# Routing, ranking and gathering tile by tile, and releasing the first expert weight slots in quarters

## The chip, the cores and the metric

The kernel runs on one core of one Trainium2 chip. The metric is the time of one execution on the device in microseconds (us); lower is better. The core's engines are named as in the profile: PE is the matrix engine, PEld its weight loads, DVE the vector engine, ACT the scalar engine, POOL the general-purpose engine, SP the engine that here only issues weight transfers (its queue is SPq).

## The reference

Two layers run over 288 tokens: 256 prompt tokens and 32 sample tokens, width 1024, all in 32-bit floats. What matters here is the end of the mixing part and the start of the mixture of experts:

```python
x = layernorm(DN_ALPHA * x + merged @ w_out)              # LN1
g_prob = softmax(x @ w_router_group); g_top, g_idx = top_k(g_prob, 1)
e_logits = (x @ w_router_expert).reshape(T, 4, 8)[:, g_idx]
e_top, e_idx = top_k(softmax(e_logits), 2); e_top /= e_top.sum()
# each token goes to experts g_idx*8 + e_idx with weights g_top*e_top
h = silu(xb @ w_e_gate[e]) * (xb @ w_e_up[e]);  out = h @ w_e_down[e]
ple_term = sigmoid(x @ w_ple_gate) * (ple @ w_ple)        # the plain branch
x = layernorm(DN_ALPHA * x + moe_out + ple_term)          # LN2
```

There are 32 experts of 512 hidden units. Each layer reads 32 x 3 matrices of 2 MiB, 192 MiB of expert weights, whatever the tokens are.

## The kernel before

**Tiles.** The tokens are three tiles of 128, 128 and 32, numbered 0, 1 and 2. The token state `x` holds a token per partition; `xT` holds it turned, so that it can be the moving or stationary side of a product over the width.

**Weights.** Every weight comes as a piece of 1 MiB (128 partitions of 8 KiB) into one of 21 slots: eight in `ring`, nine in `arena`, and four that are borrowed (`cst`, `lb`, `lnw`, `xT`). `place_pieces` fixes before the run which piece goes into which slot, and `BEFORE[n]` is the piece that stood there. SP issues the loads strictly in the order of the list (`load`, L722), and ahead of each it waits until the piece before it in that slot has been used. The experts go in eight quads of four, each quad with 24 pieces in the order gate, up, down, each in two halves `h` of four pieces (one per expert). The first 15 expert pieces of a layer fit into free slots before any expert has been computed. The sixteenth and the three behind it go into the slots of the first half of the gate weights of quad 0 (`eg`, h = 0); SP waits there for `halves_used`.

**Order of the work.** The order on each engine is written out by hand. On PE it is, from the end of the mixing on: `wo` (the product with `w_out`, columns j = 0, 1) for the tiles 2 and 0, then for tile 1 split around other steps; `t1` (turning the normalised tile, `turn_mixed`); `rt` (the router product); `plain(0, 2)`, the plain branch for columns 0 and tile 2 (`pl` is the low product, `pg` the gate product); `rk` (the rank of a token within its expert, a product of the one-hot rows `route` with a triangular matrix, L1219 to L1226); `cnt`; `X0` (gathering the tokens of quad 0 into slots, `sel` as stationary side); `ST0` (turning the choice matrix) and `XT0` (turning the gathered tokens). Then quad 0 follows: G (gate), `plain(0, 1)`, U (up), `plain(1, 0)`, hT, Y (down), `plain(1, 1)`, `plain(1, 2)`, the combine C, and the gather of quad 1. Jobs write numbered PSUM banks; `MIX_JOBS` and `expert_jobs` say which.

On DVE, `mixed` adds `wo` to `x`, `norm_mixed` does LN1 (two statistics, one aggregate, two passes over 1024 columns), `route_tile` makes `route` for one tile in 18 small steps, most of which wait for the one before, and after all three tiles the ranks are turned into positions (L2098, L2100), `choose` compares them with 0..31 for `sel`, and `weigh` makes the weighted choice.

**What couples the two parts.** A step's end is signalled by `matmuls_done` (a job on PE is done), `bank_emptied` (its bank was read), `route_out`, `sel_out` and `ln_out`. `last_use` says after which job a weight slot is free; `expert_slots` assigns free slots to expert pieces by the time at which they come free.

## Time and profile before

| what | us |
|---|---|
| median of three runs | 1708.77 (1708.17 to 1712.34) |
| the profiled execution, device time | 1707.03 |
| its span in the trace | 1705.3 |
| PE busy, DVE busy, ACT busy in the span | 1381.7, 469.4, 285.7 |
| bytes moved | 491 MB, mean 288 GB/s over the span |
| layer 0: first matmul of the experts | 381.49 |
| layer 1: the same | 1226.68 |
| layer 0: last expert piece lands | 827.7 |
| layer 1: the same | 1672.7 |

The span is 1.7 us shorter than that execution's own time, and that execution is 1.7 us below the median. A reader should look at the 40 slices of the span first: the transfer rate stands at 426 to 427 GB/s in slices 11 to 19 and again in slices 31 to 39, and it varies between 1 and 424 GB/s elsewhere. The two stretches are the expert parts of the two layers.

### The profile page before, as it was taken

Reading aid. Unit: us, or ns where it says so; the run is one execution under the profiler, and the core shown is the slowest. Engines: PE = TensorE matmul, PEld = TensorE weight load, DVE = VectorE, ACT = ScalarE, POOL = GpSimd, SP = SyncE. Lnnn points to the kernel's source line nnn. Section 1 sums busy time; section 2 is a strip of 40 time slices with the busy share of each in tenths; the row PEclk is TensorE's granted clock in tenths of the full one; section 3 lists DMA queues with packets and bytes.
Section 4 is the critical chain, followed back from the end, with each engine's and each line's share of the span. In section 5 each row is a group of like instructions: output and inputs, shape, how many; then the busy total and the mean of one; then the engine's idle time right before and its main releaser. Section 6 shows DMA issues by size and latency. Waiting matters only on the chain.

```text
span 1705.3 us, 20748 instructions
## 1 busy us (share of the span) xinstructions
PE 1381.7 (81%) x8768; PEld 645.3 (38%) x8769; DVE 469.4 (28%) x1033; ACT 285.7 (17%) x705; POOL 49.6 (3%) x95
## 2 busy tenths in 40 slices
PE   5999998999957766865597999989999667657763
PEld 3556664553412212221154666645443122212211
DVE  3241563461211111100224416625511111011004
ACT  2432323020100000000135423221201000000001
POOL 1200000000000000000021000000000000000000
PEclk9999999999988888878798999999999799789877
DMA  9302414749999999999842034148499999999992
GB/s 320 120 1 100 155 50 143 296 199 391 426 427 426 427 426 427 426 427 427 318 154 76 1 111 144 58 159 360 152 424 426 427 426 427 426 426 427 426 427 109
DMA packets 97457, 491.02 MB, mean 288 GB/s; under 512 B 9264, under 2 KB 15184, under 8 KB 47696
## 3 DMA queue, kind: packets, MB, share of 16 engines
q1 hardware_dynamic: 92608, 478.16, 68.7%
q0 software_dynamic: 4752, 11.45, 2.0%
q8 instruction: 75, 1.23, 0.3%
q14 instruction: 22, 0.18, 0.0%
HBM read 486.69 MB, written 2.89 MB: 287 GB/s over the span
## 4 chain that ended last, share of the span: by engine, by line
PE 52%; DMA 31%; SPq 10%; DVE 3%; ACT 2%; issue 2%; DVEq 0%; POOL 0%; ACTq 0%
PE bank L863 50%; SPq L722 9%; DMA lb<-in_w_e_down 6%; DMA arena<-in_w_e_gate 3%; DMA lb<-in_w_e_up 3%; DMA cst<-in_w_e_up 3%; DMA cst<-in_w_e_gate 3%; DMA arena<-in_w_e_down 3%; PE bank L898 2%; DMA xT<-in_w_e_gate 2%; DMA xT<-in_w_e_up 2%; DMA arena<-in_w_e_up 2%; DMA lb<-in_w_e_gate 2%; DMA xT<-in_w_e_down 2%; DMA ring<-in_w_in 1%
## 5 line engine op out<-in xcount | busy, mean ns | idle before, releaser
L863 PE MATMUL bank<-ring,arena 128*32 128x512 f32 (+4 forms) x1792 | 453.5, 615 | 188.1 <-DMA arena<-in_w_e_up 42.3
L863 PE MATMUL bank<-arena 128*32 128x512 f32 (+11 forms) x2648 | 531.9, 534 | 65.8 <-DMA cst<-in_w_e_gate 22.4
L863 PE MATMUL bank<-ring,xT 128*32 128x128 f32 (+5 forms) x2688 | 438.5, 374 | 4.7 <-ACT xT L1433 2.3
L863 PEld LDWEIGHTS bank<-ring,arena 128*32 128x32 f32 (+1 forms) x1792 | 136.5, 135 | 459.7 <-issue 448.4
L863 PEld LDWEIGHTS bank<-ring,xT 128*32 128x32 f32 (+1 forms) x2688 | 216.2, 138 | 196.1 <-issue 182.7
L863 PEld LDWEIGHTS bank<-arena 128*32 128x32 f32 (+5 forms) x2648 | 201.4, 142 | 211.2 <-issue 206.1
L863 PE MATMUL bank<-cst,arena 128*32 128x512 f32 (+2 forms) x240 | 122.0, 647 | 1.7 <-ACT arena L1693 1.7
L863 PE MATMUL bank<-x_sb,arena 128*128 128x512 f32 (+1 forms) x192 | 95.7, 624 | 0.6 <-DVE arena L2201 0.6
L863 PE MATMUL bank<-lb,arena 128*32 128x512 f32 x160 | 92.6, 734 | 0.0
L2181 DVE TENSOR_TENSOR arena<-arena,bank 128x512 f32<-128x512 f32 x16 | 11.0, 687 | 274.6 <-PE bank L863 274.6
L863 PE MATMUL bank<-xT,arena 128*32 128x512 f32 x128 | 77.6, 764 | 0.0
L2107 DVE TENSOR_TENSOR arena<-cst,arena 128x128 f32<-128x128 f32 (+1 forms) x48 | 10.9, 283 | 186.2 <-PE bank L863 186.1
L2189 DVE COPY arena<-bank 128x512 f32<-128x512 f32 x16 | 11.1, 691 | 168.7 <-PE bank L863 168.7
L2201 DVE TENSOR_TENSOR arena<-arena,bank 128x512 f32<-128x512 f32 (+1 forms) x80 | 49.4, 634 | 28.4 <-PE bank L863 28.3
L863 PEld LDWEIGHTS bank<-x_sb,arena 128*128 128x128 f32 (+1 forms) x192 | 31.2, 187 | 64.4 <-issue 64.4
L1689 ACT COPY arena<-bank 128x512 f32<-128x512 f32 x16 | 9.4, 585 | 257.1 <-PE bank L863 257.1
L898 PE MATMUL bank<-cst,arena 128*128 128x128 f32 (+4 forms) x296 | 37.6, 271 | 10.0 <-ACT arena L1500 5.1
L1705 ACT ACTIVATE arena<-bank 128x512 f32<-128x512 f32 x16 | 9.6, 597 | 207.5 <-PE bank L863 207.5
L898 PEld LDWEIGHTS bank<-cst,arena 128*128 128x128 f32 (+4 forms) x296 | 32.2, 149 | 20.7 <-issue 18.4
L863 PEld LDWEIGHTS bank<-cst,arena 128*32 128x32 f32 (+2 forms) x240 | 32.2, 147 | 16.8 <-issue 14.5
L1718 ACT COPY arena<-bank 128x512 f32<-128x512 f32 x16 | 9.4, 586 | 160.3 <-PE bank L863 160.3
L898 PE MATMUL bank<-cst,x_sb 128*128 128x128 f32 (+1 forms) x96 | 13.3, 285 | 27.4 <-DVE x_sb L1775 18.0
(231 smaller groups left out, 913.2 us busy)
## 6 DMA issues: line engine op xcount, KB each, us to landing
arena<-in_w_e_gate SPq DMA_DIRECT2D x64, 1024.0 KB, 26.3
arena<-in_w_e_up SPq DMA_DIRECT2D x60, 1024.0 KB, 26.5
arena<-in_w_e_down SPq DMA_DIRECT2D x58, 1024.0 KB, 26.4
ring<-in_w_e_down SPq DMA_DIRECT2D x52, 1024.0 KB, 26.5
ring<-in_w_e_up SPq DMA_DIRECT2D x48, 1024.0 KB, 26.6
ring<-in_w_e_gate SPq DMA_DIRECT2D x44, 1024.0 KB, 26.5
ring<-in_w_in SPq DMA_DIRECT2D x32, 1024.0 KB, 9.5
ring<-in_w_out SPq DMA_DIRECT2D x8, 1024.0 KB, 6.8
```

Source lines behind the costliest of these rows:

```text
L722: sp.dma_start(dst, src).then_inc(ring_full[i], 16)
L863: return pe.matmul(out, lhsT, rhs, start=first, stop=last, skip_group_check=True)
L898: ins = pe.transpose(b[0:m, a:a + src.shape[0]], src, ident[0:src.shape[0], 0:src.shape[0]])
L1689: emptied(act.copy(xg[:, 0:512], bank(key)[:, :]), key)
L1705: emptied(act.activation(eh[:, :], bank(key)[:, :], ACT.Silu), key)
L1718: emptied(act.copy(ye[:, 0:512], bank(key)[:, :]), key)
L2107: ins = dve.tensor_tensor(s4, bcast(iota[0:n, :], 1, QUAD), bcast(posm[0:n, t, first], 2, CAP), ALU.is_equal)
L2181: emptied(dve.tensor_tensor(hid[:, :], eh[:, :], bank(key)[:, :], ALU.mult), key)
L2189: emptied(dve.tensor_copy(ye[:, 512:1024], bank(key)[:, :]), key)
L2201: emptied(dve.tensor_tensor(a, a, src, ALU.add), key)
```

## The change

1. **Ranking without all tiles.** The triangular constant gets 512 on its diagonal (`RANK0`), so that the rank product gives 512 + rank for a chosen token and under 512 for another. `choose_tile` compares the ranks directly with `places` (512 to 543). The two steps that made positions fall away, and `rank(t)` for a tile needs only the tiles ahead of it in the order 2, 0, 1.
2. **Shorter routing steps.** `route_tile` masks the other groups with one operation in place of five, and the negated maxima and the second one-hot row come behind `route_out`. The clearing operations run once, ahead of the tiles.
3. **Gather without a turn.** `gather_first` multiplies `x` (stationary, 128 columns at a time) with `sel` (128 columns) and gives the turned tokens `XT0` at once: 16 products for the tiles 2 and 0 and eight for tile 1. `X0` and its copies fall away. `ST0` moves behind `plain(0, 1)` in quad 0.
4. **LN1 in pieces.** `mixed` takes the statistics of each half at once; for tile 1 the two passes run in halves, and the turn begins after the first (`x_half`). The columns of `w_out` are reordered on the host, so `x` is written contiguously.
5. **The plain branch.** `plain(0, 0)` moves from ahead of the experts to behind Y of quad 0, ahead of `plain(1, 1)`. Its two gate slots come free later, and the pieces from the 24th expert piece on are assigned to slots anew.
6. **Quarters.** The four pieces that follow the first half of G in its slots are loaded as 16 blocks of 512 columns (256 KiB, rows of 2 KiB), released by `chunks_used` after each of the first three quarters of that half and by `halves_used` after the fourth.

PE between the mixing and the first expert (`x_sb` is `x`, `wr` the router weights; rows with both `cst` and `arena` and 32 columns are ranks and counts). Before:

```order
L863 MATMUL bank<-wr,xT 128x36 x8
L863 MATMUL bank<-ring,xT 128x512 x4
L863 MATMUL bank<-ring,arena 32x128 x8
L863 MATMUL bank<-ring,xT 32x128 x32
L863 MATMUL bank<-ring,arena 128x512 x2
L898 MATMUL bank<-cst,x_sb 128x128 x8
L863 MATMUL bank<-wr,xT 128x36 x8
L863 MATMUL bank<-ring,xT 128x512 x4
L863 MATMUL bank<-arena,cst 128x32 x3
```

Now, from the same router product of tile 0 on:

```order
L900 MATMUL bank<-wr,xT 128x36 x8
L900 MATMUL bank<-ring,xT 128x512 x4
L900 MATMUL bank<-arena,cst 32x32
L900 MATMUL bank<-arena,cst 128x32 x2
L900 MATMUL bank<-ring,xT 128x512 x4
L900 MATMUL bank<-arena,x_sb 128x128 x16
L935 MATMUL bank<-cst,x_sb 128x128 x8
L900 MATMUL bank<-wr,xT 128x36 x8
L900 MATMUL bank<-ring,arena 32x128 x8
L900 MATMUL bank<-ring,xT 32x128 x32
L900 MATMUL bank<-arena,cst 128x32 x3
L900 MATMUL bank<-arena,x_sb 128x128 x8
```

The ranks of two tiles and two thirds of the gather now stand ahead of tile 1's turn, and the plain products of tile 0 are gone from here.

SP behind the first release by the experts. Before, from the 20th expert piece on (the 16th to the 19th wait for the first half of G):

```order
L722 DMA arena<-in_w_e_down 128x2048 [waits matmuls_done] x4
L722 DMA ring<-in_w_e_down 128x2048 [waits matmuls_done]
L722 DMA ring<-in_w_e_gate 128x2048 [waits matmuls_done]
L722 DMA ring<-in_w_e_gate 128x2048 [waits halves_used]
L722 DMA arena<-in_w_e_gate 128x2048 [waits halves_used] x2
```

Now, from the last blocks of the quarters on:

```order
L773 DMA arena<-in_w_e_up 128x512 [waits halves_used]
L773 DMA arena<-in_w_e_down 128x512 x2
L773 DMA cst<-in_w_e_down 128x512
L740 DMA arena<-in_w_e_down 128x2048 [waits matmuls_done] x4
L740 DMA ring<-in_w_e_down 128x2048 [waits halves_used]
L740 DMA arena<-in_w_e_gate 128x2048 [waits halves_used] x2
```

The two ring loads that waited for a plain job ahead of U are no longer there; the piece behind the four that wait for the end of G now waits for the first half of U.

The core of the diff:

```diff
-    c[:, C_TRI:C_TRI + P] = u < t
+    c[:, C_TRI:C_TRI + P] = (u < t) + RANK0 * (u == t)
...
-    j = [(("G",), 0)] + plain(0, 1, 2, 3) + [(("U",), 1)] + plain(1, 0, 7, 0)
+    j = [(("G",), 0)] + plain(0, 1, 2, 3) + ([(("ST0",), 4)] if g == 0 else []) + [(("U",), 1)] + plain(1, 0, 7, 0)
...
-    j += [(("Y", 0), 5), (("Y", 1), 6)] + plain(1, 1, 1, 2) + plain(1, 2, 3, 4) + combine
+    j += [(("Y", 0), 5), (("Y", 1), 6)] + plain(0, 0, 7, 0) + plain(1, 1, 1, 2) + plain(1, 2, 3, 4) + combine
...
-    turns += [(first_g + 1.5, i) for i in pg[0:2]] + [(first_y + 1.5, i) for i in [pl] + pg[2:4] + [XT_SLOT]]
+    turns += [(first_y + 1.2, i) for i in pg[0:2]] + [(first_y + 1.5, i) for i in [pl] + pg[2:4] + [XT_SLOT]]
...
+                def load_quarters(ks):
+
+                    for c in range(4):
+                        if c < 3:
+                            sp.wait_ge(chunks_used, 3 * layer + c + 1)
+                        else:
+                            sp.wait_ge(halves_used, 3 * QUADS * layer + 1)
+                        for k in ks:
...
+                            src = experts[w][g * QUAD + e, :, h, 512 * c:512 * c + 512]
+                            sp.dma_start(slot(n)[:, 512 * c:512 * c + 512], src).then_inc(ring_full[SLOT_OF[n]], 16)
...
+                def rank(t):
+
+                    pe.wait_ge(route_out, 3 * layer + MIX_ORDER.index(t) + 1)
+                    b = open_bank((layer, "rk", t))
+                    for k, s in enumerate(MIX_ORDER[0:MIX_ORDER.index(t)]):
+                        mm(b[0:NT[t], 0:32], ones[0:NT[s], 0:NT[t]], route[0:NT[s], s, :], k == 0, False)
+                    done(mm(b[0:NT[t], 0:32], tri[0:NT[t], 0:NT[t]], route[0:NT[t], t, :], t == MIX_ORDER[0], True))
+
+                def gather_first(tiles):
...
+                                ins = mm(b[:, c * P:(c + 1) * P], x[0:NT[t], t, k * P:k * P + P], sel[0:NT[t], t, :],
+                                         t == MIX_ORDER[0] and c == 0, t == MIX_ORDER[2])
...
                 turn_mixed(2)
-                mix(0, 1)
+                half_mix(0, 0)
...
-                half_mix(0)
+                half_mix(0, 1)
                 router(0)
-                half_mix(1)
+                half_mix(1, 0)
+                rank(2)
+                rank(0)
+                half_mix(1, 1)
+                pe.wait_ge(sel_early, layer + 1)
+                gather_first((2, 0))
+                turn_mixed(1)
+                router(1)
...
                 plain(0, 2)
-                plain_low(0, 0)
-                turn_mixed(1)
-                router(1)
-                half_gate = lambda h: project_half(layer, ("pg", 0), 0, xT, [("pg", 0, 0), ("pg", 0, 1)], h)
-                half_gate(0)
...
+                rank(1)
+                pe.wait_ge(sel_out, QUADS * layer + 1)
+                gather_first((1,))
...
+                            if name == "G":
+                                job_read(pe, (layer, "XT0", h) if g == 0 else (layer, "moe", g - 1, "XT", h))
...
+                                if name == "G" and g == 0 and h == 0 and c < 3:
+                                    ins.then_inc(chunks_used, 1)
...
-                    step(dve.tensor_scalar(r[:, 52:56], r[:, 48:52], BIG, -BIG, ALU.mult, ALU.add))
...
-                    step(dve.tensor_tensor(e4, e4, bcast(r[:, 48:52], 2, PER_GROUP), ALU.mult))
-                    step(dve.tensor_tensor(e4, e4, bcast(r[:, 52:56], 2, PER_GROUP), ALU.add))
...
+                def place_tile(t):
+
+                    key = (layer, "rk", t)
+                    job_done(dve, key)
+                    ins = choose_tile(t, bank(key)[0:NT[t], 0:QUAD])
+                    emptied(dve.tensor_copy(posm[0:NT[t], t, 0:32], bank(key)[0:NT[t], 0:32]), key)
+                    return ins
```

## Rows read from the trace of the kernel before

**Rows 1.** Stretches (from:to, length): busy by engine, PEclk, DMA share, GB/s.

```profile
365.00:385.00 20.00, 19.17 (x93) 8.45 (x95) 12.06 (x61) 5.58 (x10) 0.00 (x0) 1.00 0.02 7
...
385.00:390.00 5.00, 5.00 (x40) 1.81 (x33) 1.27 (x6) 1.36 (x2) 0.00 (x0) 1.00 0.74 267
...
480.00:800.00 320.00, 218.99 (x1313) 70.50 (x1315) 37.97 (x79) 17.19 (x32) 0.00 (x0) 0.84 1.01 427
...
830.00:835.00 5.00, 4.08 (x24) 0.90 (x16) 0.69 (x1) 0.58 (x1) 0.00 (x0) 0.68 1.07 389
```

**Rows 2.** Timeline of SP's queue, layer 0: start, us, engine, line, operation, out<-in.

```profile
360.78 0.33 SPq L722 DMA_DIRECT2D lnw<-in_w_e_up  x1
385.18 0.33 SPq L722 DMA_DIRECT2D arena<-in_w_e_up  x1
...
401.35 0.91 SPq L722 DMA_DIRECT2D arena<-in_w_e_gate  x2
...
449.04 1.24 SPq L722 DMA_DIRECT2D ring<-in_w_e_down  x2
```

**Rows 3.** Timeline of PE, layer 0, from tile 0's turn to the experts.

```profile
346.00 1.09 PE L898 MATMUL bank<-cst,x_sb 128*128 128x128 f32 x8
346.93 3.60 PE L863 MATMUL bank<-ring,xT 128*128 128x512 f32 x8
350.37 1.87 PE L863 MATMUL bank<-wr,xT 128*128 128x36 f32 x16
...
355.68 0.64 PE L863 MATMUL bank<-ring,arena 128*32 128x128 f32 x16
...
358.00 1.98 PE L863 MATMUL bank<-ring,arena 128*128 128x512 f32 x4
360.81 1.09 PE L898 MATMUL bank<-cst,x_sb 128*128 128x128 f32 x8 [0.82 <-DVE x_sb L1775]
362.73 1.95 PE L863 MATMUL bank<-wr,xT 128*128 128x36 f32 x16 [0.83 <-ACT xT L1433]
...
368.11 1.62 PE L863 MATMUL bank<-arena,cst 128*128 128x32 f32 x18
...
379.03 0.61 PE L1282 MATMUL bank<-cst,arena 128*128 128x128 f32 x3
...
381.49 0.59 PE L863 MATMUL bank<-cst,arena 128*32 128x512 f32 x1 [0.83 <-ACT arena L1693]
...
388.50 1.98 PE L863 MATMUL bank<-ring,arena 128*128 128x512 f32 x4
...
397.28 0.62 PE L863 MATMUL bank<-arena 128*32 128x512 f32 x2
```

**Rows 4.** Timeline of DVE, layer 0, tile 1.

```profile
355.79 0.69 DVE L2042 SCALAR_TENSOR_TENSOR x_sb<-x_sb,bank 128x512 f32<-128x512 f32 x1 [0.17 <-PE bank L863]
...
359.46 1.28 DVE L1775 SCALAR_TENSOR_TENSOR x_sb<-x_sb,small,lnw 128x1024 f32<-128x1024 f32 x1
361.93 0.69 DVE L1785 COPY xT<-bank 128x512 f32<-128x512 f32 x1 [1.19 <-PE bank L898]
364.72 0.15 DVE L2060 COPY arena<-bank 128x4 f32<-128x4 f32 x1 [2.10 <-issue]
...
367.86 0.19 DVE L2079 TENSOR_TENSOR arena<-arena 128x32 f32<-128x32 f32 x1
```

**Rows 5.** Timeline of PE: products of 128 columns in the recurrence of layer 0.

```profile
240.68 1.95 PE L863 MATMUL bank<-arena 128*128 128x128 f32 x16
```

**Rows 6.** Timeline of ACT, layer 0, ahead of the experts.

```profile
368.16 1.28 ACT L1673 ACT_TABLE_LOAD   x1
```

**Rows 7.** Timeline of PE, layer 1: half a gate product, and the first expert matmul.

```profile
1208.18 5.38 PE L863 MATMUL bank<-ring,xT 128*128 128x512 f32 x8
...
1226.68 0.59 PE L863 MATMUL bank<-cst,arena 128*32 128x512 f32 x1 [0.83 <-ACT arena L1693]
```

**Rows 8.** DMA issues: out<-in, engine, count, KB each, median us to landing.

```profile
lnw<-in_w_e_up SPq DMA_DIRECT2D x2, 1024.0 KB, 6.0
```

More of the change, by code:

```diff
@@ L336, in expert_slots, with first_released, in_quarters @@
     return out
+def first_released(n):
+    layer, k = divmod(n, LAYER_PIECES)
+    return len(PIECES) <= k < len(PIECES) + QUAD
+def in_quarters(n):
+    return BEFORE[n] is not None and first_released(BEFORE[n])
 def place_pieces():
@@ L348, in place_pieces @@
             slots.append(i)
+            before.append(last[i])
+            count[i] += 4 if last[i] is not None and first_released(last[i]) else 1
             fills.append(count[i])
-            before.append(last[i])
-            count[i] += 1
             last[i] = len(slots) - 1
@@ L774, in _ @@
                         load(n, 2, D, w_ple[layer].rearrange("(p c) n -> p c n", c=2))
+                ks = [k for k in range(QUADS * len(MOE_PIECES)) if in_quarters(layer * LAYER_PIECES + len(PIECES) + k)]
+                assert ks == list(range(ks[0], ks[0] + QUAD)) and ks[0] >= early_pieces
                 for k in range(early_pieces, QUADS * len(MOE_PIECES)):
-                    load_expert(k)
+                    if k == ks[0]:
+                        load_quarters(ks)
+                    if k not in ks:
+                        load_expert(k)
         @block.gpsimd
@@ L1184, in router @@
                 def router(t):
-                    for h in range(2):
-                        job_read(pe, (layer, "t1", t, h))
                     b = open_bank((layer, "rt", t))
                     for c in range(8):
+                        if c % 4 == 0:
+                            job_read(pe, (layer, "t1", t, c // 4))
                         ins = mm(b[0:NT[t], 0:36], xT[:, c, T0[t]:T0[t] + NT[t]], wr[:, c, :], c == 0, c == 7)
@@ L1286, in _ @@
                 first = layer * LAYER_PIECES + len(PIECES)
-                pe.wait_ge(sel_out, QUADS * layer + 1)
-                gather([(layer, "X0", h) for h in range(2)])
-                pe.wait_ge(selw_out, QUADS * layer + 1)
-                transpose_choice((layer, "ST0"))
-                turn_tokens([(layer, "X0", h) for h in range(2)], [(layer, "XT0", h) for h in range(2)])
                 for g in range(QUADS):
@@ L1295, in _ @@
                     turned = [key("XT", h) for h in range(2)]
-                    for h in range(2):
-                        job_read(pe, (layer, "XT0", h) if g == 0 else (layer, "moe", g - 1, "XT", h))
                     def first_layer(name, m):
@@ L1344, in _ @@
                     if g == 0:
+                        plain(0, 0)
                         plain(1, 1)
@@ L1707, in _ @@
                         plain_gate(0, 1)
+                        read_choice((layer, "ST0"))
                         plain_gate(1, 0)
```

153 lines of the change are left out of this document (88 added, 65 removed), and 7 rows, old and new, of the table MIX_JOBS.

## The prediction, made before the changed kernel had run

> **What bounds the kernel.** I read the stretches first. From 480 to 800 us the core moves 427 GB/s without a gap while PE is busy for 219 of 320 us [rows 1]: the expert part waits for weights, and a piece of 1 MiB (1.0486 MB) takes 1.0486 / 0.427 = 2.456 us. So its end is the moment at which the stream starts for good plus a fixed number of bytes, and nothing that PE or DVE save inside it counts. Then I looked for the start. From 365 to 385 us the transfers stand at 7 GB/s although PE is busy for 19.2 of 20 us [rows 1]. SP's queue says why: the fifteenth expert piece goes out at 360.78, and the next one only at 385.18 [rows 2], 3.69 us after the first expert matmul at 381.49 [rows 3]. All slots are full until the first half of G has been used. **The path is therefore: PE and DVE up to the first expert, the release, then the stream.** In the 5 us from 385 the core moves 267 of 427 GB/s, so the bytes start at 386.9, 1.7 us behind the issue [rows 1].
>
> **When the first expert starts now.** I walk PE from tile 0's turn. Steps are start to start [rows 3]: a turn 0.93 (346.00 to 346.93), a half product 3.44 (to 350.37), a router product 1.8, `plain(0, 2)` 2.32 (355.68 to 358.00), a rank or count pass 0.09 (1.62 / 18). One half of `wo` now stands behind tile 0's turn instead of ahead, so that turn starts at 346.00 - 3.44 = 342.56. LN1 of tile 0 loses one statistic and is ready by 342.2, so I charge no wait. Then: turn 343.5; half 346.9; router 348.7; half 352.15; ranks of the tiles 2 and 0, six passes, 352.7; last half of `wo` 356.15. The route of tile 0 starts at 348.8 and needs 2.55 us (below), so it is there before rank(0). The early gather is 16 products of two passes at 1.95 / 16 = 0.122 us [rows 5], 3.9 us, to 360.05; that work stands exactly where LN1 of tile 1 runs.
>
> LN1 of tile 1 took 355.79 to 360.74 on DVE, 4.95 us [rows 4]. One statistic of 0.6 us now comes earlier, since it runs while PE is at the second half. It starts 0.1 us behind PE's last half of `wo`, at 356.25, and ends at 360.7, its first half at 360.05. The turn so runs 360.1 to 361.4. Before, the router waited for DVE's copy, which ended at 362.62 [rows 4]; now that copy ends at 362.15, the first four products start earlier, and the router ends at 363.4. The route took 364.72 to 368.05, 3.33 us [rows 4]; without a copy, a mask and two products over 32 columns, and with the negations and the second one-hot row behind the signal, I count 2.55 us: 366.0. PE does `plain(0, 2)` from 363.35 to 365.65 beside it, so 0.4 us of wait is open. Then come rank(1), six passes, to 366.6; DVE's compare, 0.25 us, PE at 366.95; eight products, 1.95 us, to 368.9; the counts, 0.5 us. **G starts at 369.5** if ACT has copied the first half of the tokens by then. ACT has to get through a table load of 1.28 us [rows 6] and the gate of tile 2 after the route signal of 366.4, and is done at about 369.4: the two are level, and this is the tightest join. That is 12.0 us ahead of 381.49. The gather over 512 columns, the turn of its result and 8.8 us of `plain(0, 0)` have left this path, and the plain part comes back below.
>
> **When the stream starts.** G lasts 7.0 us (381.49 to 388.50) [rows 3]; a quarter of its first half is 0.88 us. SP issued 0.2 us behind its release before. So the first block goes out at 369.5 + 1.1 = 370.6 against 385.18, and the bytes flow at 372.3 against 386.9: 14.6 us earlier. Rows of 2 KiB are not in the expert part before. Their cost is bounded by the stretch 830 to 835 us, where weights of 2 KiB rows run at 389 GB/s, and by the 427 GB/s of 8 KiB rows [rows 1]: 4.19 MB take 10.8 or 9.8 us. I take 10.8, the like row.
>
> **Whether it keeps flowing.** This is where I think part of the gain goes. From the sixteenth piece on, 29 pieces and the 1 MiB of LN2 rows can move before one waits for the first half of G of quad 1: 30 x 2.456 = 73.7 us. Before, the stream had work until 386.9 + 73.7 = 460.6, and that release came at 449.04 [rows 2], ready at 450.7: 9.9 us to spare. Now the work lasts until 372.3 + 73.7 + 1.0 = 447.0. The release was 67.55 us behind the start of G. It gets the choice's turn (0.55 us) and `plain(0, 0)`, 8.78 us as `plain(0, 1)` shows (388.50 to 397.28) [rows 3], and comes 76.9 us behind G: issue at 446.4, bytes at 448.1. **The stream stands still for 1.1 us, and the piece after the gap flows at 448.1 instead of 460.6: 12.5 us.** Behind it PE needs far less time for a quad than the 58.9 us of its bytes, so the gain stays. An earlier join holds: after eight pieces (372.3 + 20.6 = 392.9) the next waits for the first half of U, issued 19.86 us behind G before (401.35) [rows 2], now 20.4, bytes at 391.6. By this ledger the quarters are worth only about 1 us of the 12.5: without them the stream would start at 374.9 and run dry at 448.6, half a microsecond behind the same release. The release of quad 1 sets the result.
>
> **Layer 1** has the same steps, but before it lost time at a lower clock: half a gate product took 5.38 us against 3.60 [rows 3, 7], behind a wait for LN1. If that dip is gone, layer 1 gains 14.3; if one falls there again, 12.5. PE's waits at that join shrink from 1.65 us to some tenths, so I take the middle, 13.4.
>
> **Sum.** 12.5 + 13.4 = 25.9 us, against an execution of 1707.03 us: 1681.1. The median stood 1.7 us above that execution, so the median is 1708.8 - 25.9 = 1682.9. What runs after the last piece (last products, combine, LN2, outputs) is unchanged.
>
> **The rivals.**
>
> *The release of quad 1 is in time.* If `plain(0, 0)` or the start of G comes a little sooner, or the 2 KiB rows hold the stream up longer than the gap, the earlier bytes count in full: up to 14.6 and 16.4 us, 1677.8. For it: the gap is a difference of two sums of 75 us and only 1.1 us. Chance 0.14.
>
> *The new chain of tile 1 waits more.* Route, rank, compare, gather and ACT's copy follow each other without cover; `plain(0, 2)` is the only filler of 2.3 us, where 3.4 us of half a gate stood before. Each hand-over was 0.1 us in the rows; with 3 us more in all in each layer, G starts at 372.5 and the gain is 9.5 + 10.4: 1688.9. Chance 0.19.
>
> *PE is slower in quad 0.* It is on the path now up to the release of quad 1. In the stretch 480 to 800 us its granted clock is 0.84 [rows 1], behind idle times; at 0.92 over the 76.9 us the release is 6.7 us later in each layer: 1708.8 - 12.5 = 1696.3. Against it: the clock was 1.00 from 365 to 390 us [rows 1]. Chance 0.08.
>
> *Blocks of 256 KiB break the stream.* A lone piece lands 6.0 us after its issue [rows 8], of which 2.46 are its bytes, so 3.5 us are not. If each of the 16 blocks paid that by itself, the stream would be 56 us longer and run dry at 502 instead of 460.6: 41 us lost per layer, 1708.8 + 83 = 1792. It becomes a loss from 0.85 us a block on. Against it: pieces in a full queue follow each other at 427 GB/s although each pays that latency, so the latencies overlap, and four blocks are released at a time. Chance 0.03. The Trainium skill, "DMA: Bandwidth & Descriptors", section "Bandwidth", advises transfers of at least 1 MiB and speaks against blocks of 256 KiB; by the fixed 2.0 us per transfer that its section "Anatomy of one DMA" gives, 16 blocks would cost 32 us where nothing overlapped, an estimate that would make each layer some 17 us slower than before. The 427 GB/s of the full queue disagree with such a sum for 1 MiB pieces; no row shows it for blocks.
>
> *It does not do what it says.* If the new slots let an earlier load wait for something that comes late (a plain slot ahead of the quarters in SP's order), the stream would start as before and the time stays at 1708.8. The list of loads shows only waits for G and U there. Chance 0.02.
>
> **How the numbers follow.** The forecast has the rest, 0.54, with 1679 to 1687: t0 earlier or later by 1 us in each layer, and the clock dip in or out. The range of 8 in 10 takes in most of the first two rivals: 1676 to 1692. A measurement here can tell about 0.3%, 5 us, from no change. Faster by more than that: the forecast and the first three rivals, 0.95; within it 0.02; slower 0.03.
>
> **What would show it.** In the new profile: the first expert matmul at 369.5 (368.5 to 371) in layer 0; first block issued 1.1 us behind it; 20 us of 7 GB/s shrunk to 7 us; all four quarters' bytes in 10 to 11 us; `plain(0, 0)` between Y and the combine, G of quad 1 at 73.2 us behind G of quad 0; a short hole in the transfers at about 447 us, and none after. Wrong would be: no hole (then the release was in time and the time is below 1680), a hole ahead of U's pieces at 391 us, or PE waiting more than 1 us ahead of the gather of tile 1.

## The result

The changed kernel took 1679.76 us, the median of four runs (1677.59 to 1681.78); the kernel before, on the same chip, 1709.38 (1708.17 to 1712.34). The ratio is 0.9825, with a 95% interval of 0.9812 to 0.9839. The forecast was 1682.9 us. The profiled execution of the changed kernel took 1681.78 us with a span of 1680.0, so its span is 25.3 us under that of the kernel before. The two medians stand 29.6 us apart.

PE from the turn of tile 0 to the first expert, layer 0, is the answer to [rows 3]. Columns as there: start, duration in us, then the group, and in brackets the idle time ahead of it and what ended it.

```profile
341.40 1.09 PE L935 MATMUL bank<-cst,x_sb 128*128 128x128 f32 x8
...
347.47 3.68 PE L900 MATMUL bank<-ring,xT 128*128 128x512 f32 x8
351.08 0.92 PE L900 MATMUL bank<-arena,cst 32*32 32x32 f32 x6
351.83 3.68 PE L900 MATMUL bank<-ring,xT 128*128 128x512 f32 x8
355.44 4.41 PE L900 MATMUL bank<-arena,x_sb 32*128 32x128 f32 x32
359.69 1.13 PE L935 MATMUL bank<-cst,x_sb 128*128 128x128 f32 x8
361.06 1.95 PE L900 MATMUL bank<-wr,xT 128*128 128x36 f32 x16 [0.24 <-ACT xT L1492]
362.93 0.65 PE L900 MATMUL bank<-ring,arena 128*32 128x128 f32 x16
...
365.70 0.96 PE L900 MATMUL bank<-arena,cst 32*128 32x32 f32 x6 [0.38 <-DVE arena L2144]
367.05 2.05 PE L900 MATMUL bank<-arena,x_sb 128*128 128x128 f32 x16 [0.38 <-DVE arena L2154]
369.03 0.42 PE L900 MATMUL bank<-arena,cst 128*1 128x32 f32 x6
369.38 0.62 PE L900 MATMUL bank<-cst,arena 128*32 128x512 f32 x1
```

The first expert product, called G from here on, starts at 369.38 instead of 381.49. The engine waits three times, 1.0 us in all, where [rows 3] showed 2.5 us (0.82, 0.83 and 0.83).

SP's queue, as in [rows 2]: the first block, the twelfth, the first whole pieces behind the blocks, and the first load that the second quad releases.

```profile
370.50 0.33 SPq L773 DMA_DIRECT2D arena<-in_w_e_up  x1
...
376.60 0.43 SPq L773 DMA_DIRECT2D cst<-in_w_e_down  x1
...
379.76 2.23 SPq L740 DMA_DIRECT2D arena<-in_w_e_down  x4
...
445.35 0.33 SPq L740 DMA_DIRECT2D ring<-in_w_e_down  x1
```

The stretches, as in [rows 1] (from:to, length, busy by engine, granted clock, DMA share, GB/s):

```profile
365.00:370.00 5.00, 4.24 (x48) 3.24 (x44) 2.07 (x11) 3.88 (x7) 0.00 (x0) 1.00 0.05 16
370.00:372.50 2.50, 2.50 (x31) 0.74 (x24) 2.00 (x13) 0.13 (x1) 0.00 (x0) 1.00 0.34 98
372.50:375.00 2.50, 2.50 (x31) 0.70 (x27) 2.16 (x13) 0.00 (x0) 0.00 (x0) 1.00 0.93 299
375.00:377.50 2.50, 2.50 (x19) 0.89 (x12) 1.21 (x6) 0.96 (x2) 0.00 (x0) 1.00 0.90 275
377.50:380.00 2.50, 2.50 (x8) 1.06 (x7) 0.00 (x0) 0.92 (x1) 0.00 (x0) 1.00 0.97 336
380.00:382.50 2.50, 2.50 (x8) 1.06 (x7) 0.00 (x0) 0.00 (x0) 0.00 (x0) 1.00 1.04 386
382.50:385.00 2.50, 2.50 (x7) 1.09 (x6) 0.00 (x0) 0.00 (x0) 0.00 (x0) 1.00 1.09 430
...
480.00:800.00 320.00, 217.69 (x1300) 69.83 (x1296) 36.10 (x75) 16.82 (x31) 0.00 (x0) 0.85 1.01 427
```

The expert part is as before: 427 GB/s, with PE busy for 218 of 320 us. The start is not what the forecast had. The blocks begin to flow early, but in the 10 us from 372.5 at only 275 to 386 GB/s. And at 447 us nothing stands still:

```profile
446.00:447.00 1.00, 1.00 (x16) 0.42 (x12) 0.00 (x0) 0.00 (x0) 0.00 (x0) 1.00 0.99 418
447.00:448.00 1.00, 1.00 (x15) 0.32 (x8) 0.00 (x0) 0.00 (x0) 0.00 (x0) 1.00 1.06 451
```

Layer 1 has the same row for its first expert product, at 1202.01 against 1226.68 [rows 7]:

```profile
1202.01 0.62 PE L900 MATMUL bank<-cst,arena 128*32 128x512 f32 x1
```

### The profile page after: what moved, and what is told of

It reads as the page before. It is cut to its first block, busy times and chain, and to the rows that moved or that the text cites. A ratio compares the mean times of both kernels' runs of the same rounds, so it can differ in the third digit from the quotient of the medians.

```text
span 1680.0 us, 20858 instructions
## 1 busy us (share of the span) xinstructions
PE 1371.4 (82%) x8824; PEld 649.8 (39%) x8825; DVE 466.2 (28%) x1012; ACT 284.6 (17%) x703; POOL 49.7 (3%) x95
## 4 chain that ended last, share of the span: by engine, by line
PE 54%; DMA 34%; SPq 6%; DVE 3%; ACT 2%; issue 1%; DVEq 0%; POOL 0%; ACTq 0%
PE bank L900 51%; DMA arena<-in_w_e_up 10%; DMA arena<-in_w_e_down 8%; SPq L740 6%; DMA xT<-in_w_e_down 3%; DMA lb<-in_w_e_up 3%; PE bank L935 2%; DMA lb<-in_w_e_down 2%; DMA cst<-in_w_e_down 2%; DMA xT<-in_w_e_up 2%; DMA cst<-in_w_e_gate 2%; DMA cst<-in_w_e_up 2%; DMA ring<-in_w_in 1%; DVE x_sb L1845 0%; DVE arena L1840 0%
## 5 line engine op out<-in xcount | busy, mean ns | idle before, releaser
L900 PE MATMUL bank<-ring,arena 128*32 128x512 f32 (+4 forms) x1760 | 515.9, 605 | 220.5 <-DMA arena<-in_w_e_up 45.4
L900 PE MATMUL bank<-arena 128*32 128x512 f32 (+8 forms) x2680 | 524.2, 530 | 24.2 <-DVE arena L2265 14.2
L900 PEld LDWEIGHTS bank<-ring,arena 128*32 128x32 f32 (+1 forms) x1760 | 146.0, 135 | 526.8 <-issue 518.7
L900 PEld LDWEIGHTS bank<-arena 128*32 128x32 f32 (+3 forms) x2680 | 199.9, 142 | 131.5 <-issue 126.6
L900 PE MATMUL bank<-lb,arena 128*32 128x512 f32 x160 | 86.7, 693 | 0.0
L900 PE MATMUL bank<-x_sb,arena 128*128 128x512 f32 x168 | 83.9, 625 | 0.6 <-DVE arena L2278 0.6
L2154 DVE TENSOR_TENSOR arena<-small,arena 128x128 f32<-128x128 f32 (+1 forms) x42 | 9.6, 283 | 157.1 <-PE bank L900 157.1
L900 PEld LDWEIGHTS bank<-x_sb,arena 128*128 128x128 f32 x168 | 27.1, 187 | 56.4 <-issue 56.4
L2056 DVE TENSOR_REDUCE arena<-arena 128x128 f32<-128x1024 f32 (+1 forms) x24 | 34.6, 1440 | 1.9
```

What stands on the lines that cost most here:

```text
L900: return pe.matmul(out, lhsT, rhs, start=first, stop=last, skip_group_check=True)
L2056: dve.reduce_sum(att[0:n, h, 0:n], a[0:n, :, :].rearrange("p l t -> p t l"), AX.X).then_inc(att_out, 1)
L2154: return dve.tensor_tensor(s4, bcast(places[0:n, :], 1, QUAD), bcast(ranks, 2, CAP), ALU.is_equal)
```

## The experiments

To compare executions, each is cut at three kinds of event in both layers: M, the first product of the mixing (at 318.96 in the changed kernel); G, the first expert product; L, the landing of the layer's last expert piece. So what an execution lost or gained ahead of a stretch does not count in it. All in us:

| kernel | to M | M to G | G to L | L to M | M to G | G to L | span |
|---|---|---|---|---|---|---|---|
| before | 320.1 | 61.36 | 446.2 | 336.1 | 62.87 | 446.0 | 1705.3 |
| e8, before again | 319.3 | 62.87 | 446.3 | 337.2 | 62.88 | 446.3 | 1707.4 |
| e12, before, filled | 319.3 | 62.86 | 446.4 | 337.2 | 62.87 | 446.0 | 1707.1 |
| after | 319.0 | 50.42 | 446.1 | 336.2 | 50.42 | 445.8 | 1680.0 |
| e1, after again | 320.3 | 50.41 | 445.6 | 334.1 | 50.42 | 446.0 | 1680.5 |
| e11, after again | 320.4 | 50.42 | 445.9 | 333.2 | 50.43 | 445.5 | 1678.4 |
| e2, whole pieces | 318.8 | 50.42 | 446.0 | 336.3 | 50.42 | 446.0 | 1681.7 |
| e3, halves | 320.3 | 50.42 | 445.3 | 333.8 | 50.42 | 444.7 | 1677.9 |
| e10, halves again | 320.0 | 50.43 | 445.3 | 333.3 | 50.42 | 444.6 | 1677.1 |
| e4, longer quad 0 | 318.6 | 50.42 | 451.4 | 333.5 | 50.42 | 451.1 | 1688.8 |
| e5, plain first | 319.0 | 58.75 | 445.3 | 334.6 | 58.75 | 445.3 | 1695.5 |
| e6, late gather | 318.7 | 60.11 | 446.2 | 336.6 | 60.20 | 445.1 | 1699.5 |
| e7, long route | 320.4 | 52.70 | 445.8 | 333.8 | 52.69 | 445.1 | 1683.9 |
| e9, long route, filled | 318.6 | 51.17 | 445.1 | 336.5 | 51.17 | 445.0 | 1679.6 |

M to G repeats to 0.1 us in every kernel but the one before (61.36 once, 62.87 five times). G to L repeats to about 1 us: e1, e7, e9 and e11 load the same blocks as the changed kernel, and it takes 445.0 to 446.1 in them. The stretches ahead of M, which no edit of an experiment touches, differ between executions of one kernel by 1.5 and 3 us. So the sizes below are read from M to G and G to L, and a difference of 2 us between two spans says nothing by itself.

**e1, e8: both kernels again, no edit.**

> The changed kernel once more. The two profiled executions differ by 25.3 us of span, the timed medians by 29.6 us. If the difference between these two comes from what single executions draw (clock dips of the matrix engine), a new profile has its first expert matmul again at 369.4 and 1202 us give or take 1.5, and its span anywhere between 1675 and 1681. Rival: the timed runs hold something that the profiled one does not; then the median stays near 1679.8 and the span of the new profile stays at 1680.0 or above.

> The kernel before once more. Segments: m0 to G0 61.4 and 62.9 us, G0 to last landing 446.2 and 446.0. If the 1.5 us between the layers is a clock dip that single executions draw, it may be gone or stand in the other layer; if it belongs to the wait ahead of tile 1's turn, it is there again in layer 1. The stretch from the last landing of layer 0 to m0 of layer 1, 336.1 us here, was 333.5 to 336.3 in five executions of the changed kernels: the same spread is expected.

The changed kernel again: 1681.43 us (four runs, 1680.43 to 1684.98) against 1708.54, ratio 0.9844 (0.9827 to 0.9861). The span of this profile, 1680.5, lies where both sides of its expectation allow it, and decides nothing between them. The kernel before again, one execution: 1709.14 us, span 1707.4. Its layer 0 had the slow gate product that the forecast had seen in layer 1 only:

```profile
363.70 5.38 PE L863 MATMUL bank<-ring,xT 128*128 128x512 f32 x8
```

and the granted clock, third column from the end, stands at half there:

```profile
364.00:366.00 2.00, 2.00 (x4) 0.69 (x3) 1.73 (x12) 0.00 (x0) 0.00 (x0) 0.53 0.22 90
```

e12 below has this dip in both layers too, so the profiled execution of the kernel before looks like the exception, as far as three profiles can tell. If it was, 1.5 us of the difference of the medians are not in the difference of the spans.

**e2: the four pieces whole.** Every other edit stays.

```diff
-    return BEFORE[n] is not None and first_released(BEFORE[n])
+    return False
...
-            count[i] += 4 if last[i] is not None and first_released(last[i]) else 1
+            count[i] += 1
...
-                    if k == ks[0]:
-                        load_quarters(ks)
-                    if k not in ks:
-                        load_expert(k)
+                    load_expert(k)
```

> The changed kernel, but the four pieces behind the first half of the gate weights are loaded whole, released together as before. Theory A (ledger of bytes): the first issue comes 3.7 us behind the first expert matmul instead of 1.1, so bytes start at 374.8 instead of 372.2, but at 427 GB/s at once. The quarters moved 4.5 MB in the 12.8 us from 372.2 on, as if at full rate from 374.4. So the whole pieces lose only 0.4 us a layer, 0.8 us in all. Rival B: the earlier start counts in full, 2.6 us a layer, 5.2 us in all.

1682.74 us, ratio 0.9847 (0.983 to 0.9863). G to L is 446.0 in both layers, against 445.5 to 446.1 in the six layers of the changed kernel (after, e1, e11): a mean of 0.2 us apart, where the expectation had 0.4 and its rival 2.6. The median is 1.3 us above that of e1 on the same chip, with ranges that overlap. So the quarters are worth little, if anything. The reason stands in the stretches:

```profile
372.50:375.00 2.50, 2.50 (x28) 0.78 (x24) 2.16 (x13) 0.00 (x0) 0.00 (x0) 1.00 0.45 79
375.00:377.50 2.50, 2.50 (x19) 0.81 (x8) 1.08 (x6) 1.08 (x2) 0.00 (x0) 1.00 0.96 397
377.50:380.00 2.50, 2.50 (x7) 1.14 (x6) 0.00 (x0) 0.80 (x1) 0.00 (x0) 1.00 1.00 423
```

Whole pieces start 2.5 us later and are at 397 and 423 GB/s at once, where the quarters stand at 275 and 336. Summed over such stretches, 12 us behind G of layer 0 there have moved 2.81 MB with whole pieces (e2) and 3.03 to 3.17 MB with quarters (after, e1, e11): of a lead of 2.5 us, 0.5 to 0.8 is left there, and at the landing it can't be told from none.

**e3 and e10: halves instead of quarters**, with e11, the changed kernel, as e10's partner on one chip.

```diff
...
-                    for c in range(4):
-                        if c < 3:
-                            sp.wait_ge(chunks_used, 3 * layer + c + 1)
+                    for c in range(2):
+                        if c < 1:
+                            sp.wait_ge(chunks_used, layer + 1)
...
-                            src = experts[w][g * QUAD + e, :, h, 512 * c:512 * c + 512]
+                            src = experts[w][g * QUAD + e, :, h, 1024 * c:1024 * c + 1024]
...
-                                if name == "G" and g == 0 and h == 0 and c < 3:
+                                if name == "G" and g == 0 and h == 0 and c == 1:
```

> The changed kernel with two blocks of 1024 columns (512 KiB, rows of 4 KiB) per piece in place of four of 512 columns, released after the second and the fourth quarter of that half. Theory A: the slow first 10 us of the quarters come from the size of rows and blocks. With 4 KiB rows near 427 GB/s the first issue 1.95 us behind the first expert acts as full rate from about 373.1, 1.3 us ahead of the quarters; it is cut to about 1.0 us a layer by the release of quad 1 (ready at 447.05, the stream would be dry at 446.7). 2 us faster in all. Rival B: the loss is that of the first issues after an idle queue, whatever the size; then it is the same as the quarters or 0.9 us a layer slower.

> The first four pieces of the expert stream in halves of 512 KiB, the same kernel as e3, beside the changed kernel (e11) on one chip. If halves are better than quarters: from the first expert product to the landing of the last piece 444.7 to 445.3 us in both layers, against 445.6 to 446.1 with quarters, and the timed median 1 to 2.5 us under that of e11. If the 2.5 us between e3 and e1 were the head and the dense stages of one execution: both medians within 0.7 us. Against the kernel before 0.9826 give or take 0.001.

> The changed kernel a third time, as the partner of e10. Expected 1679.5 to 1682 us timed, 50.42 us from the first mixing product to the first expert product in both layers, and 445.6 to 446.1 us from there to the landing of the last piece. A ratio to the kernel before of 0.983 to 0.985; the same stretch lengths as in the two profiles of it so far would show that what differs between its executions lies in the head and in the dense stage of layer 1.

e3 took 1678.93 us (1678.46 to 1679.67), ratio 0.9826 (0.9809 to 0.9842), where e1 on the same chip took 1681.43. e10 took 1678.32 (1677.76 to 1679.04), ratio 0.982 (0.9807 to 0.9833), and e11 1680.18 (1679.68 to 1681.58), ratio 0.9833 (0.982 to 0.9847), five runs each. G to L is 444.6 to 445.3 in the four layers with halves and 445.5 to 446.1 in the six of the changed kernel, 0.8 us apart in the mean. Halves start 1.1 us later than quarters and then catch up:

```profile
375.00:377.50 2.50, 2.50 (x28) 0.65 (x20) 1.71 (x9) 0.00 (x0) 0.00 (x0) 1.00 1.00 388
377.50:380.00 2.50, 2.50 (x10) 1.12 (x7) 0.68 (x3) 1.88 (x2) 0.00 (x0) 1.00 1.03 411
```

12 us behind G they have moved 3.35 and 3.31 MB, 0.5 MB more than whole pieces, which is 1.2 us. This is the fastest version: its median stands 2.5 and 1.9 us under that of the changed kernel on the same chip, and in neither pair do the ranges of the two overlap. That is less than the 5 us which the forecast took as the least that can be told from no change. The landing alone does not carry it: the layers with quarters in e5, e6, e7 and e9 take 445.0 to 446.2 from G to L, and six of these eight are at 445.3 or below. What carries the difference is that the timed medians show it on two chips, and that the bytes moved by 12 us behind G are more in both profiles of halves than in any of quarters or whole pieces.

Why the first blocks are slow stays open; the size of the blocks and the length of their rows (2, 4 and 8 KiB) were changed together. Neither caps the rate by itself: the last 0.7 MB of the changed kernel's 4.19 MB of blocks move in 382.50 to 385.00, a stretch at 430 GB/s. Nor did the stream wait for SP: by 377.03 SP had issued twelve blocks, 3.15 MB, and by 377.38 1.66 MB had moved.

**e4: eight more products in quad 0**, in the middle of `plain(0, 0)`. Their sum is overwritten.

```diff
-                        plain(0, 0)
+                        plain_low(0, 0)
+                        b = open_bank((layer, "pg", 0, 0))
+                        for c in range(8):
+                            mm(b[:, :], xT[:, c, 0:P], slot(piece_number(layer, ("pg", 0, 0)))[:, 0:512], True, True)
+                        plain_high(0, 0)
```

> The changed kernel with eight more products of 512 columns on the matrix engine ahead of the gate product of plain(0, 0) in quad 0, about 7.1 us, overwritten by the real ones. Theory A: the release of quad 1 had about 1.0 us to spare (ready at 447.05 against a stream that runs dry at 448.0), so a hole of 6.1 us opens at about 448 us and the whole is 12.2 us longer. Rival B: quad 0 has slack of more than 7 us, no hole, same time. Rival C: the release was already on the path, 14.2 us longer.

1690.89 us, ratio 0.9898 (0.9882 to 0.9915). The group `411.40 7.03 ... x16` of the changed kernel now reads, in PE's timeline:

```profile
411.06 13.90 PE L900 MATMUL bank<-ring,xT 128*128 128x512 f32 x32
```

6.87 us more work. SP's first load into a slot that the second quad frees goes out at 451.88 instead of 445.35, and here the hole is:

```profile
446.00:448.00 2.00, 1.90 (x12) 1.19 (x11) 0.76 (x2) 0.90 (x2) 0.00 (x0) 1.00 0.90 381
448.00:449.00 1.00, 0.82 (x8) 0.34 (x12) 0.63 (x1) 0.98 (x2) 0.00 (x0) 1.00 0.29 123
...
450.00:452.00 2.00, 2.00 (x24) 0.69 (x20) 0.00 (x0) 0.00 (x0) 0.00 (x0) 1.00 0.00 0
452.00:453.00 1.00, 1.00 (x16) 0.41 (x12) 0.00 (x0) 0.00 (x0) 0.00 (x0) 1.00 0.70 98
```

The stream runs dry at about 448, and G to L is 5.6 and 5.3 us longer than the mean of the changed kernel's six layers (445.8). So of 6.87 us some 1.2 to 1.6 us were slack and the rest counts in full; the expectation had 1.0 us of slack. By the medians e4 is 9.5 us above e1, where 12.2 was expected and G to L gives 10.9. That release is the next limit of this kernel, as the forecast said, but the changed kernel stands just inside of it.

**e5: `plain(0, 0)` ahead of the experts again**, with its slots as early as before, everything else as changed.

```diff
...
                 plain(0, 2)
+                plain(0, 0)
                 rank(1)
...
                     if g == 0:
-                        plain(0, 0)
                         plain(1, 1)
...
```

> The changed kernel, but plain(0, 0) stands ahead of the experts again (between plain(0, 2) and rank(1)), with its gate slots free at their old place. Segments from the first matmul of the mixing (m0) to the first expert matmul (G0), now 50.4 us in both layers. Theory A (the matrix engine's queue is the path there, all but 0.8 us of waits): 8.8 us more work less those waits, so m0 to G0 is 58.4 us; G0 to the landing of the last piece stays at 446.0, since release of quad 1 comes 8.8 us earlier relative to G0 and had been in time already. 16 us in all. Rival B: the gain of the change came from the shorter route and the early gather, and the plain branch was hidden; then it is within 3 us.

1697.21 us against 1709.47, ratio 0.9929 (0.9912 to 0.9946). M to G grows by 8.33 us in both layers. PE's timeline shows the work that comes back:

```profile
365.27 1.98 PE L901 MATMUL bank<-ring,arena 128*128 128x512 f32 x4
367.09 7.03 PE L901 MATMUL bank<-ring,xT 128*128 128x512 f32 x16
```

G to L is 0.5 us shorter in the mean; whether that is because quad 0 has less to do is not shown, since e9 with all of quad 0 takes 445.0. So moving these two jobs is worth two thirds of the 12.45 us a layer. The other 4.1 are what all other edits bring together, the 1.5 us of the dip in the kernel before among them: in e5 the clock is 1.00 from 358 to 378 us.

**e6: the gather of the tiles 2 and 0 behind tile 1's ranks**, where the gather of tile 1 is.

```diff
                 half_mix(1, 1)
-                pe.wait_ge(sel_early, layer + 1)
-                gather_first((2, 0))
                 turn_mixed(1)
...
                 pe.wait_ge(sel_out, QUADS * layer + 1)
+                gather_first((2, 0))
                 gather_first((1,))
```

> The changed kernel, but all 24 products of the first gather stand behind the rank of tile 1. Theory A: the 16 early ones run in the time in which LN1 of tile 1 runs on the vector engine (they end 0.3 us behind it), so moving them leaves a hole there: m0 to G0 is 4.1 us longer, 54.5, and 8.2 us in all. A second effect, if idle time lowers the clock behind the hole: up to 2 us more in a layer. Rival B: only their order changes, the same work in the same time; then below 1 us.

1700.42 us, ratio 0.9948 (0.9931 to 0.9964). M to G grows by 9.7 us, where the expectation had 4.1 and at most 2 more for the clock. Taking 4.25 us of work from under LN1 of tile 1 and putting it behind explains under half of that. PE's timeline shows where the rest is:

```profile
359.21 1.67 PE L935 MATMUL bank<-cst,x_sb 128*128 128x128 f32 x8 [3.99 <-DVE x_sb L1844]
360.67 3.56 PE L900 MATMUL bank<-wr,xT 128*128 128x36 f32 x16
...
367.77 0.96 PE L900 MATMUL bank<-arena,cst 32*128 32x32 f32 x6
369.11 9.38 PE L900 MATMUL bank<-arena,x_sb 32*128 32x128 f32 x48 [0.38 <-DVE arena L2153]
```

And the stretches, whose third column from the end is the granted clock:

```profile
360.00:364.00 4.00, 4.00 (x20) 3.88 (x20) 0.69 (x1) 1.42 (x7) 0.00 (x0) 0.50 1.01 403
...
368.00:370.00 2.00, 1.62 (x14) 1.47 (x13) 0.39 (x2) 1.34 (x2) 0.00 (x0) 1.00 0.00 0
...
372.00:376.00 4.00, 4.00 (x18) 3.61 (x17) 0.00 (x0) 0.00 (x0) 0.00 (x0) 0.50 0.00 0
```

The clock is at half, 1.2 GHz, twice. It falls first behind the wait of 3.99 us: the router takes 3.56 us instead of 1.95, and the steps from the turn to the ranks lose 2.5 us. The Trainium skill, "TensorE: Matmul & The Clock Gate", section "HAM oscillation — how this bites in real kernels", tells of the same chain, a wait and then work at half clock; the rows of this first fall agree on that. Then it is back at full from 368 to 370, the ranks take their 0.96 us, and it falls again in the gather, whose 48 passes take 9.38 us instead of 4.41 + 2.05, some 3.1 us more from start to start. Ahead of this second fall stands a wait of 0.38 us, no longer than that of the changed kernel, which has no fall there. So its cause is not shown. At full clock M to G would have grown by 4.1 us; 5.6 us are the clock.

**e7: the long routing steps**, the five masking operations and the copy, with the negation and both one-hot rows ahead of the signal.

```diff
-                    step(dve.tensor_copy(lg[:, 0:4], b[0:n, 0:4]))
+                    dve.tensor_copy(lg[:, 0:4], b[0:n, 0:4])
+                    emptied(dve.tensor_copy(lg[:, 8:40], b[0:n, 4:36]), key)
...
+                    step(dve.tensor_scalar(r[:, 52:56], r[:, 48:52], BIG, -BIG, ALU.mult, ALU.add))
+                    step(dve.tensor_tensor(e4, e4, bcast(r[:, 48:52], 2, PER_GROUP), ALU.mult))
+                    step(dve.tensor_tensor(e4, e4, bcast(r[:, 52:56], 2, PER_GROUP), ALU.add))
...
```

> The changed kernel with the old steps in route_tile (mask by five operations, negated maxima and both one-hot rows ahead of the signal). Theory A: only tile 1's route is on the path; it took 3.33 us before and 2.6 now, so m0 to G0 is 0.7 us longer, 51.1, in both layers. Rival B: the routes of the tiles 2 and 0 delay the early ranks as well; they ended 0.7 us ahead of the ranks on the matrix engine, so at most 0.3 us more.

One execution: 1685.71 us. M to G grows by 2.28 us in both layers, more than either side of the expectation had (0.7 and 1.0), where the steps themselves are 0.74 us longer. PE's timeline of e7:

```profile
367.84 0.96 PE L900 MATMUL bank<-arena,cst 32*128 32x32 f32 x6 [1.12 <-DVE arena L2149]
369.19 3.58 PE L900 MATMUL bank<-arena,x_sb 128*128 128x128 f32 x16 [0.38 <-DVE arena L2155]
```

and one stretch of it, at half clock:

```profile
370.00:372.00 2.00, 2.00 (x11) 2.00 (x11) 0.00 (x0) 0.68 (x2) 0.00 (x0) 0.50 0.00 0
```

The wait ahead of tile 1's ranks is 1.12 us instead of 0.38, and the gather behind it takes 3.58 us instead of 2.05: 0.74 + 1.53 = 2.27. Whether the wait or something else lowered the clock was open, so:

**e9: e7 with 12 more products in that wait** (24 passes, 0.65 us), their sums overwritten.

```diff
-                plain(0, 2)
+                plain_low(0, 2)
+                w = slot(piece_number(layer, ("pl",))).rearrange("p (c n) -> p c n", c=2)
+                b = open_bank((layer, "pg", 0, 2))
+                for c in range(3):
+                    for cols, out in cuts(b, 2):
+                        mm(out, xT[:, c, T0[2]:T0[2] + NT[2]], w[:, 0, cols], True, True)
+                plain_high(0, 2)
                 rank(1)
```

> The long routing steps again, with 12 more products of the size of a gate piece on TensorE between the last router and tile 1's ranks, so that the engine works through most of the wait that the long steps left it there (1.12 us in e7, 0.38 us in the changed kernel). Their sums are overwritten by the gate products that follow. Theory A, the granted clock halved in e7 because TensorE stood there: the 1.12 us shrink to about 0.4, the gather of tile 1 takes 2.05 us again instead of 3.58, and from the first mixing product to the first expert product it is 51.2 us in both layers (50.42 in the changed kernel plus the 0.74 us of longer steps), at most 51.6 if the extra products outlast the wait. Theory B, the halving has another cause than the wait: the gather keeps its 3.6 us and the stretch is 52.7 us or longer. By A the more work is the shorter stretch.

One execution: 1681.41 us. M to G is 51.17 us in both layers, 1.53 less than e7 with more work:

```profile
366.11 0.96 PE L900 MATMUL bank<-arena,cst 32*128 32x32 f32 x6 [0.47 <-DVE arena L2155]
367.46 2.05 PE L900 MATMUL bank<-arena,x_sb 128*128 128x128 f32 x16 [0.38 <-DVE arena L2161]
```

At this place the wait that the long steps leave is the cause, shown by filling it with work and leaving the long steps. So the short steps are worth 0.74 us of time and 1.53 us of clock in each layer.

The sizes from e5, e6 and e7 don't add up to the gain, nor should they: 8.3, 9.7 and 2.3 us are what is lost when one edit is taken out of the changed kernel, while the kernel before had other work in the waits that then open. LN1 in pieces has no run of its own.

**e12: the kernel before with one of its waits filled.** Two more passes stand ahead of `plain_low(0, 0)`, again without effect on what is computed.

```diff
+                w = slot(piece_number(layer, ("pl",))).rearrange("p (c n) -> p c n", c=2)
+                b = open_bank((layer, "pl", 0, 0))
+                mm(b[:, :], pT[:, 0, 0:P], w[:, 0, 0:512], True, True)
                 plain_low(0, 0)
```

> The kernel before with one more product of 128x512 (two passes, 0.86 us by the rows of its plain gate) on TensorE ahead of the plain gate's products of tile 0, so that the engine works through the 0.82 us in which it waits for tile 1's normalised rows; its sum is overwritten. The wait of 0.83 us for tile 1's turned columns stays. Theory A, these two waits within 2.8 us are why the granted clock falls to half for the gate products behind them (5.38 us for 8 instead of 3.68 in e8, both layers): the 5.38 us become 3.68, and from the first mixing product to the first expert product it is 61.4 us in both layers instead of 62.87; more work, 1.5 us less time. Theory B, the fall comes from something else at this place: the 5.38 us stay, and the stretch is 62.9 us.

One execution: 1708.92 us. The wait of 0.82 us is gone, and the dip stays, in both layers:

```profile
357.13 2.84 PE L863 MATMUL bank<-ring,arena 128*128 128x512 f32 x6
...
361.85 1.95 PE L863 MATMUL bank<-wr,xT 128*128 128x36 f32 x16 [0.83 <-ACT xT L1436]
363.63 5.38 PE L863 MATMUL bank<-ring,xT 128*128 128x512 f32 x8
```

Theory A falls in this form: the first wait is not needed for the dip of the kernel before. The second, 0.83 us, was not filled. That one, where the changed kernel has 0.24, may be the cause alone; against it stands that the profiled execution of the kernel before had both waits in layer 0 and no dip [rows 3]. What makes this dip stays open. With e6's second fall, behind a wait of 0.38 us, these are two places where the length of the wait ahead does not tell whether the clock falls.

## Why the prediction was right, and where its steps were not

**What bounds the kernel: right.** The expert part flows at 427 GB/s in both kernels, and from M to G 12.45 us a layer went away, or 10.9 where the dip was missing. Every kernel that started G later ended later by about as much: e5 (8.33 us a layer) came out 15.8 us above e1, e6 (9.7) 19.0 us, both on another chip than e1.

**First expert product at 369.5: read 369.38, by luck, since two errors cancel.** From tile 0's turn to G the working had 26.9 us (342.56 to 369.5) and the trace has 28.0 (341.40 to 369.38). The steps that were priced too low are, for tile 1, the one from its ranks to its gather, 1.35 us instead of 0.9; and ahead of it the early gather, 4.25 instead of 3.9, the ranks of two tiles, 0.75 instead of 0.55, and two half products of `wo`, 3.61 each instead of 3.45. The last gather and the counts, 2.33 instead of 2.55, give a little back. What hid the sum is not in the working at all: the profiled execution reached M 1.2 us earlier than that of before. e1 and e11 reach M at 320.3 and 320.4, and their G stands at 370.7 and 370.8. A pass of the early gather takes 4.25 / 32 = 0.133 us instead of the 0.122 of [rows 5]. The working let DVE start when PE could issue the next product, 0.55 us behind the first rank pass; the trace has it start when the six passes are through, 0.96 us behind. The join called the tightest, ACT's copy, was ready about 0.5 us ahead:

```profile
368.24 0.59 ACT L1751 COPY arena<-bank 128x512 f32<-128x512 f32 x1
```

**First block 1.1 us behind G: right**, 370.50 - 369.38 = 1.12.

**4.19 MB of blocks at 389 GB/s: the mis-sized term.** The price came from weights with 2 KiB rows in the dense stage [rows 1]. That stretch is no clean source for it: of the 3096 packets from 820 to 836 us, 2163 were under 2 KB. The blocks ran at 275 to 336 GB/s in the 7.5 us up to 380. By 381.38 us 3.03 MB had moved, where 389 GB/s from 372.3 on give 3.53: 0.5 MB or 1.2 us less. The blocks so cost some 2.2 us more than whole pieces at full rate, not 1.0. The quarters' worth, which the forecast put at about 1 us of the 12.5 (its own two times, 448.6 and 448.1, give 0.5), is 0.2 from G to L.

**A hole of 1.1 us at 447: wrong, by this term and one more.** With the slower blocks the stream runs dry at 447.0 - 0.1 + 1.2 = 448.1. And the release was issued at 445.35, 75.97 us behind G where 76.9 was forecast, and so ready at 447.05. Of these 0.9 us some 0.5 are a wait that the sum took over from the kernel before: PE stood 0.83 us ahead of the second quad's gate product there, and now it reads

```profile
441.66 0.62 PE L900 MATMUL bank<-arena 128*32 128x512 f32 x2 [0.28 <-issue]
```

The rest is `plain(0, 0)` and the choice's turn, 8.58 and 0.39 us instead of 8.78 and 0.55. Either error by itself would have left a hole of under 0.2 us. The forecast's own sign of being wrong, no hole and a time below 1680, came true (1679.76). The rival in which this release is in time so happened as a mechanism, but without its gain: the late bytes of the blocks took what the missing hole gave. 12.5 us at the stream was right for layer 0; the landing of the last piece moved by 12.3 us. e4 shows that the limit is real from 1.2 to 1.6 us on.

**Layer 1: 13.4 forecast, 12.7 measured** between the two profiles at the last landing (1672.7 to 1647.8, less the 12.3 of layer 0): 12.45 from M to G, where the dip of before is gone, and 0.2 from G to L. The working had a stream start 2.6 us earlier than G explains, of which the blocks gave back nearly all.

**The sum: 25.9 forecast, 25.3 between the spans, 27.1 to 29.6 between the medians** of three comparisons. Of what the medians have beyond the spans, 1.5 us is the dip in layer 0 that e8 and e12 show in the kernel before. Some 0.5 us is G to L: the means of three profiles each, 446.2 and 445.8, are 0.8 us apart in two layers, the two profiled executions 0.35. The rest, where there is one, lies in the stretches ahead of M, in the dense stage between the layers, 336.1 to 337.2 us in the three profiles of the kernel before and 333.2 to 336.6 in the others; its values fall in two heaps, 333.2 to 334.6 and 336.1 to 336.6. No run here explains them, and it stays open whether the change has a part in it.

**The other rivals.** The chain of tile 1 waits more: PE's waits there are 1.0 us in all, not 3 more than before. PE slower in quad 0: the clock was 1.00 in all stretches from 360 to 480, so over all of quad 0. Blocks of 256 KiB break the stream: no, but they start it slowly, which is the true part of that rival, at 2.2 us over the full rate instead of 56. By the fixed 2.0 us per transfer that the Trainium skill gives in "DMA: Bandwidth & Descriptors", section "Anatomy of one DMA", for transfers issued from the general-purpose engine, the 16 blocks, here issued by SP, would have cost 32 us one behind the other, an estimate; they cost 2.2, so the measurement disagrees with that sum where several blocks are in flight. An earlier load that waits for something late: there is none, the first block goes out 1.1 us behind G.

## What to carry to other kernels

Where a stream of transfers bounds a stage, find the release that starts it, and count only what lies ahead of that release; then look for the next release that the earlier stream will reach, since the slack there is all that a further gain or a further piece of moved work can use (1.2 to 1.6 us here). Work that fills a wait on TensorE can be worth more than its own time: the early gather gave 4.1 us by its place and 5.6 us by the clock that it kept. Blocks that are released early pay only while their lead is longer than their slower start, so of the three cuts tried two blocks a piece was the best, not four.

## What the runs showed of the hardware

- Waits of 1.12 us (e7) and 3.99 us (e6) on TensorE were followed by stretches at a granted clock of 0.50. A wait of 0.47 us at the place of the first (e9) was not. In e6 the clock came back to 1.00 for 368 to 370 us and fell again to 0.50 behind a wait of only 0.38 us. In the kernel before a dip of 1.5 us stood behind a wait of 0.83 us in five of six layers, and not in the sixth.
- 16 blocks of 256 KiB, issued as their slots came free behind an empty queue, moved at 275 to 386 GB/s for 10 us, and the last of them in a stretch at 430. Eight blocks of 512 KiB reached 388 to 411, and pieces of 1 MiB 397 to 423, in the first whole stretches behind their start.
